# The first modulation rows of a two-block transformer kernel, loaded and summed in three column chunks instead of one

## The reference, cut to what matters

```
c_act = silu(c)                                  # 2048 numbers
mod   = c_act @ w_ada + b_ada                    # w_ada: 2048 x 12288, float32
sh1, sc1, gt1, sh2, sc2, gt2 = split(mod, 6)     # 2048 each
h = rms_norm(x, g_mix) * (1 + sc1) + sh1
z = h @ w_in                                     # w_in: 2048 x 11344
```

## Time and profile before

| | |
|---|---|
| three runs | 2665.74, 2667.66, 2667.6 us |
| the profiled execution | 2666.06 us, of it span 2664.2 us |
| TensorE matmul busy | 2625.6 us (99%) |
| VectorE busy | 1798.2 us (67%) |
| ScalarE busy | 1297.8 us (49%) |
| read from memory | 582.07 MB, 219 GB/s over the span |

### The profile page before, as it was taken

How to read it: one execution, slowest core, us unless ns; L and a number is a source line. 1 busy time by engine, 2 the same in 40 slices (tenths; PEclk the granted TensorE clock), 3 DMA queues, 4 the chain that set the end, 5 groups by cost and what they waited for, 6 DMA issues and landing times.

```text
span 2664.2 us, 33329 instructions
## 1 busy us (share of the span) xinstructions
PE 2625.6 (99%) x12045; PEld 2164.4 (81%) x12045; DVE 1798.2 (67%) x2072; ACT 1297.8 (49%) x1574; POOL 230.2 (9%) x164
## 2 busy tenths in 40 slices
PE   5999999999999999999999999999999999999999
PEld 3888887888888888888888887887888888888887
DVE  7978777878776677776766855677555555555554
ACT  4455544455454444444444554556454444444443
POOL 0000000100000000000001210240001111111110
PEclk9999999999999999999999999999999999999999
DMA  9989768678867766666665666644666666666663
GB/s 382 401 308 340 243 209 281 196 237 283 304 211 241 220 220 219 218 218 216 218 195 177 198 178 181 190 143 132 199 186 193 190 189 189 190 190 191 191 191 134
DMA packets 280792, 585.61 MB, mean 220 GB/s; under 512 B 22033, under 2 KB 24493, under 8 KB 279797
## 3 DMA queue, kind: packets, MB, share of 16 engines
q1 hardware_dynamic: 280340, 583.61, 68.1%
q10 hardware_dynamic: 352, 0.71, 0.1%
HBM read 582.07 MB, written 2.11 MB: 219 GB/s over the span
## 4 chain that ended last, share of the span: by engine, by line
PE 96%; DVE 2%; DMA 1%; ACT 0%; issue 0%; DVEq 0%; ACTq 0%
PE lin L499 30%; PE lin L501 30%; PE lin L500 30%; DMA sb_ada<-in_w_ada_dram 1%; PE aux L812 1%; PE aux L499 1%; PE aux L501 1%; PE aux L500 1%; PE aux L533 1%; PE aux L986 0%; PE aux L823 0%; DVE sb_wlo L1617 0%; DVE sb_acc L1708 0%; PE aux L557 0%; PE aux L999 0%
## 5 line engine op out<-in xcount | busy, mean ns | idle before, releaser
L1617 DVE TENSOR_TENSOR sb_wlo<-sb_raw,sb_whi 128x1024 fp32r<-128x1024 f32 x896 | 1114.8, 1247 | 784.8 <-ACT sb_whi L1041 781.2
L1041 ACT ACTIVATE sb_whi<-sb_raw 128x1024 fp32r<-128x1024 f32 x896 | 948.9, 1060 | 1237.2 <-PE lin L501 1159.1
L499 PE MATMUL lin<-sb_whi,sb_act_hi 128*128 128x512 f32 x2620 | 1038.4, 396 | 1.9 <-DVE sb_wlo L1617 1.0
L501 PE MATMUL lin<-sb_whi,sb_act_lo 128*128 128x512 f32 x2620 | 1021.8, 390 | 0.0
L500 PE MATMUL lin<-sb_wlo,sb_act_hi 128*128 128x512 f32 x2620 | 1020.7, 390 | 0.0
L499 PEld LDWEIGHTS lin<-sb_whi,sb_act_hi 128*128 128x128 f32 x2620 | 492.5, 188 | 108.5 <-issue 9.3
L501 PEld LDWEIGHTS lin<-sb_whi,sb_act_lo 128*128 128x128 f32 x2620 | 492.1, 188 | 104.3
L500 PEld LDWEIGHTS lin<-sb_wlo,sb_act_hi 128*128 128x128 f32 x2620 | 492.7, 188 | 99.9 <-issue 1.9
L499 PE MATMUL lin<-sb_whi,sb_hid_hi 128*128 128x512 f32 x704 | 275.3, 391 | 0.0
L501 PE MATMUL lin<-sb_whi,sb_hid_lo 128*128 128x512 f32 x704 | 274.1, 389 | 0.0
L500 PE MATMUL lin<-sb_wlo,sb_hid_hi 128*128 128x512 f32 x704 | 274.0, 389 | 0.0
(11 more groups left out here) (362 smaller groups left out, 1819.5 us busy)
## 6 DMA issues: line engine op xcount, KB each, us to landing
sb_raw<-in_w_in_dram SPq DMA_DIRECT2D x176, 512.0 KB, 6.7
sb_raw<-in_ffn_w_gu_dram SPq DMA_DIRECT2D x176, 512.0 KB, 3.7
sb_ada_in<-in_w_ada_dram SPq DMA_DIRECT2D x128, 512.0 KB, 5.1
sb_raw<-in_gla_w_in_dram SPq DMA_DIRECT2D x96, 512.0 KB, 3.8
sb_raw<-in_w_gate_dram SPq DMA_DIRECT2D x88, 512.0 KB, 3.8
sb_raw<-in_w_up_dram SPq DMA_DIRECT2D x88, 512.0 KB, 4.4
sb_raw<-in_w_down_dram SPq DMA_DIRECT2D x88, 512.0 KB, 4.4
sb_raw<-in_ffn_w_down_dram SPq DMA_DIRECT2D x88, 512.0 KB, 3.6
```

What stands on the lines that cost most here:

```text
L499: pe.matmul(o, h, whi[:, w], start=first and q == 0, stop=False)
L501: m = pe.matmul(o, l, whi[:, w], start=False, stop=last and q == 1)
L1041: act.activation(whi[:, idx % RING * HALF:(idx % RING + 1) * HALF], raw[:, idx // 2 % RING, idx % 2 * HALF:(idx % 2 + 1) * HALF], ACT.Copy ...
L1617: dve.tensor_tensor(wlo[:, c], raw[:, idx // 2 % RING, idx % 2 * HALF:(idx % 2 + 1) * HALF], whi[:, c].bitcast(fp32), ALU.subtract).then_i ...
```

## The change

**Row pieces.** The columns of the six early blocks are cut in three chunks of two blocks. A row piece is now `[128, 2 x 256]`, 256 KB, and there are 48: 16 for each chunk, chunk after chunk. The slots are still six, so piece n waits until piece n - 6 has been used.

**Who sums them.** 25 pieces (`TENSOR_ROWS`) are multiplied by TensorE: four matmuls of a 128 x 128 block by one column of c, added up in PSUM (`row_columns`, L626). The other 23 are added by VectorE as before, 512 columns wide (`row_add`, L1785, L1787). `chunk_columns` adds VectorE's accumulator to the same PSUM columns. Eight of TensorE's pieces stand ahead of the turns of x, three between them, and 14 in front of the matmuls of halves 0 to 6 (`ROWS_BEHIND`). VectorE's pieces of chunks 1 and 2 stand behind the splits of halves 0 to 6 (`ADDS_AT`).

**Order of halves.** The first three groups begin pair by pair: halves 0 to 2 are pair 0 of three groups, 3 to 5 pair 1, 6 to 8 pair 2; from half 9 on it is group after group as before. The modulation of pair 1 is made at half 3, that of pair 2 at half 6.

**SyncE's queue.** x is first, then 8 pieces, half 0, 8 pieces, half 1, and so on; late pieces begin after half 7 instead of half 4, the late sums are turned into columns behind half 39 instead of half 38. VectorE scales one of the two token blocks of x. The `keep_running` matmuls and the parameter loads ahead of phase A are gone or moved behind half 8 and half 12.

Between the splits of halves 5 and 6 now stand four adds (pieces 37, 38, 40 and 41), between that of half 6 and the modulation three (43, 44 and 46); ahead of the split of half 5 there are two (34 and 35). The core of the diff:

```
+CHUNKS = ((0, 2), (2, 4), (4, EARLY), (EARLY, KT))
+ROWS_BEHIND = {0: (17, 19), 1: (21, 23), 2: (25, 27), 3: (29, 31), 4: (33,), 5: (36,), 6: (39, 42, 45, 47)}
+ADDS_AT = {0: (16, 18), 1: (20, 22), 2: (24, 26, 28, 30), 3: (32,), 4: (34, 35), 5: (37, 38, 40, 41), 6: (43, 44, 46)}
+PIECES_FROM = (0, 8, 16, 24, 32, 37, 42, 48)
...
+        def row_piece(n):
+            if n >= SLOTS:
+                row_taken(n - SLOTS)
+            kt, c = n % KT, n // KT
+            sp.dma_start(ada0[:, n % SLOTS, :].rearrange("p (b n) -> p b n", b=2), w_first[kt * P:(kt + 1) * P, :, 2 * c * P:2 * (c + 1) * P]
+                         ).then_inc(sem(f"ada0_in{n % SLOTS}"), 16)
+        def row_taken(n):
+            if n in TENSOR_ROWS:
+                sp.wait_ge(sem("ada0_T"), row_on_tensor(n))
+            else:
+                sp.wait_ge(sem("ada0_sum"), VECTOR_ROWS.index(n) + 1)
...
+        sp.dma_start(X[:], tokens(A["x"][0])).then_inc(sem("x_in"), 16)
+        for n in range(PIECES_FROM[1]):
+            row_piece(n)
+        for i in range(A_ENDS[-1]):
+            first_half(i)
+            if i + 2 < len(PIECES_FROM):
+                for n in range(PIECES_FROM[i + 1], PIECES_FROM[i + 2]):
+                    row_piece(n)
...
+        def row_columns(n):
+            kt, c = n % KT, n // KT
+            pe.wait_ge(sem(f"ada0_in{n % SLOTS}"), 16 * (n // SLOTS) + 16)
+            if all(m >= n for m in TENSOR_ROWS if m // KT == c):
+                pe.matmul(column_banks[c][:, 0:4], ident, nothing, start=True, stop=False)
+            for j in range(4):
+                m = pe.matmul(column_banks[c][:, j:j + 1], ada0[:, n % SLOTS, j * P:(j + 1) * P], cact[:, kt:kt + 1], start=False, stop=False)
+            m.then_inc(sem("ada0_T"), 1)
...
+            for n in ROWS_BEHIND.get(i, ()):
+                row_columns(n)
+            if i in (A_HELD, 2 * A_HELD):
+                chunk_columns(i // A_HELD)
+            if p == made:
+                made += 1
+                pe.wait_ge(sem("tt_lo"), made)
+            half(0, "A", A_ENDS[-1], i, 0, 2 * p, first, last, banks=banks)
...
+        for g in range(A_PAIRS):
+            hk.setdefault(A_HELD * g, []).append(lambda g=g: early_pair(g))
+        for i, adds in ADDS_AT.items():
+            for n in adds:
+                hk.setdefault(i, []).insert(len(hk.get(i, ())) - (i == 6), lambda n=n: row_add(n))
```

More of the change, by code:

```diff
@@ L254, in build_program @@
     csg = small[:, 96:112]
+    nothing = small[:, 184:188]
     ss, ssy = small[:, 112:114], small[:, 114:116]
@@ L313, in ada_chunk @@
             if n < 2:
[L314 removed]
+                sp.wait_ge(sem("gs_made"), 4)
             if before >= 0:
@@ L363, in _ @@
                 sp.dma_start(relb[:], A["rel_bias"]).then_inc(sem("rel_in"), 16)
[L364 to L368, removed]
+            if LATE_FROM <= i < LATE_FROM + 2 * KT:
+                late_piece(i - LATE_FROM)
+            if i == 32:
                 sp.wait_ge(sem("erow_held"), 1)
@@ L565, in _, with chunk_columns, late_columns @@
         pe.wait_ge(sem("par_cols"), 1)
[L566 to L583, removed]
+        column_banks = (lin[0][1], aux[0], aux[1], aux[1])
+        def row_columns(n):
[6 more added lines that the diff above has]
+            m.then_inc(sem("ada0_T"), 1)
+        def chunk_columns(c):
+            pe.wait_ge(sem("ada0_sum"), sum(n < (c + 1) * KT for n in VECTOR_ROWS))
+            for j in range(4):
+                b, k = j // 2, 2 * c + j % 2
+                m = pe.matmul(column_banks[c][:, j:j + 1], acc0[:, b, k * P:(k + 1) * P], ones[:, 0:1], start=False, stop=j == 3)
+            m.then_inc(sem("ada0_T"), 1)
+        def late_columns():
+            pe.wait_ge(sem("ada0_sum"), EARLY_ROWS + 2 * KT)
+            pe.wait_ge(sem("par_cols"), 2)
+            pe.wait_ge(sem("erow_held"), 1)
+            for j in range(2 * LATE):
+                c = j % LATE * P
+                m = pe.matmul(aux[1][:, j * (WIDE // 4):(j + 1) * (WIDE // 4)], acc1[:, j // LATE, c:c + P], ones[:, 0:WIDE // 4], start=True, stop=True)
             m.then_inc(sem("ada0_T"), 1)
@@ L589, in keep_running, with late_parameters @@
                 pe.matmul(lin[0][0][:], ident, con[:, 0:NB], start=True, stop=True)
[L591 to L600, removed]
+        def late_parameters():
+            pe.wait_ge(sem("par_in"), 8 * 16)
+            for n, rws in ((1, 120), (2, 116)):
+                m = pe.transpose(aux[0][:, n % 2 * P:n % 2 * P + rws], parr[0:rws, n, :], ident[0:rws, 0:rws])
+            m.then_inc(sem("par_T"), 1)
+            pe.wait_ge(sem("rel_in"), 32)
+            pe.matmul(aux[1][0:NH, :], relb[:], onehot[:], start=True, stop=True).then_inc(sem("par_T"), 1)
+        pe.wait_ge(sem("csg_made"), 2)
+        for n in TENSOR_ROWS[:8]:
+            row_columns(n)
+        pe.wait_ge(sem("xs_made"), 2)
+        for g in range(KT // 2):
+            turn(X, g)
+            if g in (1, 3, 5):
+                row_columns(TENSOR_ROWS[8 + g // 2])
+        chunk_columns(0)
+        pe.wait_ge(sem("tt_free"), KT // 2)
         def project_ix():
@@ L654, in _ @@
         first_banks = (lin[1], lin[0], aux[2:4])
[L655 to L666, removed]
+        made = 0
+        for i, (g, p, a, first, last) in enumerate(A_HALVES):
+            n = a - A_DRAINS
+            banks = lin[n % 2] if n >= A_HELD else first_banks[a % 3]
+            if first and a >= 3:
+                pe.wait_ge(free0, A_DRAINS + 1 + n if n >= A_HELD else a)
+                pe.wait_ge(free1, A_DRAINS + 1 + n if n >= A_HELD else a)
+            for n in ROWS_BEHIND.get(i, ()):
+                row_columns(n)
+            if i in (A_HELD, 2 * A_HELD):
[4 more added lines that the diff above has]
+            half(0, "A", A_ENDS[-1], i, 0, 2 * p, first, last, banks=banks)
+            if i == 12:
+                late_parameters()
             if i == LATE_SUMMED:
-                pe.wait_ge(sem("ada0_sum"), EARLY_ROWS + 2 * KT)
-                first_columns(2)
-            if i == A_ENDS[0] - 1:
+                late_columns()
+            if i == A_ENDS[0]:
                 project_ix()
-            if i == A_ENDS[0] + 2:
+            if i == A_ENDS[0] + 3:
                 wix_turn()
```

169 lines of the change are left out of this document (85 added, 84 removed).

## The result

The changed kernel takes 2708.5 us (median of six runs, 2707.9 to 2710.1) against 2667.4 for the kernel before: ratio 1.0157, 95% interval 1.0146 to 1.0167. That is 41 us slower. The direction was forecast, the size was not: 2691 was expected and 2700 was the end of the range.

The account below looks back on a forecast made before the run. TensorE, 99% busy, was taken as the bound, so its waits cost in full. Half 6 16.9 to 22.9 us later, plus 1.7 clock and 1.5 VectorE, gave 20.1 to 26.1; 25 taken, 2691 us, range 2677 to 2700.

Parts of the forecast that it names:

- x: Start: x, now first in SyncE's queue, lands at about 10.6 us and is scaled at 18.8.
- The eight pieces: TensorE ahead of the turns of x: 0.90 or 1.8 us each, ending at 19.7 or 25.7, the second taken.
- The turns: Start, up to ScalarE's last copy: 6.4 us for turning x plus 2.7 for three pieces between, ending at 28.8 to 34.8.
- the late end: Half 0's start, forecast at 33.8 to 39.8 us: the later figure, with the eight pieces at the lower clock.
- TensorE's 14 pieces among these halves mostly lie in those waits: Halves 0 to 6: TensorE's pieces, 0.9 to 1.8 us each, mostly fall in waits for halves.
- Landing 4.4: Halves 2 to 6: each lands 4.4 us after issue, 3.7 with a nearly free queue plus 0.67 for one piece ahead.
- the steps: Half 0 to half 6: chain of issues, landings, splits and adds through six slots and one queue, 47.8 us.
- Behind half 6: After half 6 begins: 1.7 us lost to the lower clock, 1.5 to VectorE's pace (2.82 a half against TensorE's 2.73).
- the late end of the steps: Half 6's start, forecast 16.9 to 22.9 us later than before (81.6 to 87.6 against 64.72): the larger figure.
- Pieces slower than their rows: Rival, halves 0 to 8: one-column matmuls at the lower clock, each pair change throws it back; +33 to +40, 2703; chance 0.07.
- Slots free in time: Rival, pieces 16 to 47: SyncE never stops, half 6 at 68.8, or 56 to 62 if more hides, 2661; chance 0.08.
- The signs: Next profile: half 0 at 33 to 40, half 3 near 55, half 6 past 78, TensorE wait over 8, DMA not full.

Follow-up runs that it names:

- both: Changed kernel with twelve slots for row pieces instead of six and halves 0 to 6 issued ahead of piece 16: 2687.6 us, ratio 1.0078.
- warm: Changed kernel with four filler matmuls of 512 columns on TensorE after the constants land, ahead of the first eight pieces: 2710.0 us, ratio 1.0161.
- free_33_39: Changed kernel with row pieces 33 and 39 added by VectorE instead of multiplied by TensorE: 2702.2 us, ratio 1.0135.
- start_vec: Changed kernel with one row piece on TensorE ahead of half 0 instead of eleven, VectorE adding the other fifteen: 2699.0 us, ratio 1.0119.
- hold: Changed kernel with filler matmuls of 384 columns in TensorE's waits ahead of halves 3, 5 and 6: 2702.5 us, ratio 1.0133.
- spread: Changed kernel with ten row pieces on TensorE, twelve slots, pieces 0 to 15 ahead of half 0, then four between halves: 2673.9 us, ratio 1.0025.
- small_packets: Kernel before with each of sixteen early row pieces loaded as three transfers with 1 KB runs instead of one with 3 KB: 2671.7 us, ratio 1.0016.
- wide_hold: Changed kernel with two chunks, 16 + 16 pieces, seven on TensorE, twelve slots, filler ahead of halves 0 and 3, late pieces from half 4: 2669.8 us, ratio 1.0010.

## Why the prediction fell short

The mechanism was in the main the one forecast: SyncE's queue, the slots and the landings tie half 6 down, and taking that away (`both`) brings back 21 of 41 us. What was wrong is which engine lets a slot go last, and the clock at which TensorE works in this stretch. The sum was 25 and the loss 43 by the profiles. Step by step:

*x.* Scaled at 19.8, forecast 18.8. Right but for 1 us.

*The eight pieces.* They end at 26.8, forecast 19.7 or 25.7 with the second taken. Right in size, and only half for the reason given, an engine that comes from idling. In those rows the turns themselves came to the upper rate; here 64 records of one column did not, and in `warm`, where the engine did not come from idling, the clock fell under them.

*The turns: failed, 3.4 us.* I took 6.4 us from rows 9 and three pieces at 0.9. Both were prices of the upper clock, in a stretch that stands behind 13 us of one-column matmuls; measured are 12.5 us up to ScalarE's last copy, pieces included, against 9.1. If eight pieces were slow, what follows them could not be counted as fast. Half 0 came at 43.8, 4.0 behind the late end.

*"TensorE's 14 pieces among these halves mostly lie in those waits": failed, 7.4 us.* I looked at what the pieces cost TensorE and priced it at nothing. What they cost is the slot: piece 33 is multiplied behind half 3, which runs at the lower clock after its wait (5.0 us from 65.36 on), and piece 39, so half 5, stands behind it; piece 39 behind half 5 does the same to piece 45 and half 6. The prediction named VectorE's adds, of 34 and 35 and of 37 to 41, as the last releases; TensorE was later both times, and at half 3 too, where piece 25 lets piece 31 go (54.02 us in the chain). `free_33_39` shows it for 33 and 39.

*Landing 4.4: failed, about 4 us.* The lone half of rows 12 and one piece ahead was too little. While half 5 was on its way (72.97 to 78.57) the windows count 1.5 MB, nearly three times its bytes, at 230 to 340 GB/s: pieces issued on either side share the engines. With the late releases of 33 and 39 gone the loop takes 54.1 us (`free_33_39`), against 47.8 by the steps, 6.3 more. The landings of halves 4, 5 and 6 stand in its chain (6.2, 4.7, 6.3 instead of 4.4), 4.0 of these. Another 2.5 come ahead of half 4's issue, 16.1 us behind half 0 instead of 13.6, and there the chain goes through TensorE and not through a landing: half 0 at the lower clock (4.8 us) and the pieces in front of halves 1 to 3. The column sum takes 1.9 instead of 0.9; other steps were 1.2 shorter. All this is read from one run's times; the landings were not varied alone, so their share is argued and not shown.

*Behind half 6.* One stretch at the lower clock, 2.7 instead of 1.7; VectorE's pace, 0 instead of 1.5. Together near the forecast, by luck. By luck too the moved parameter loads are not seen: their matmuls behind half 12, priced at nothing, cost 1.3 us, and the kernel before lost about as much between halves 29 and 37.

So 22.9 (the late end of the steps) + 4.0 (half 0) + 7.4 + 6.3 is the 40.6 at half 6, plus 2.7.

*The rivals.* "Pieces slower than their rows" (2703, chance 0.07) came nearest in size and is half true: at the start the pieces run at the lower rate, among the halves two pieces take 1.84 us behind a half at the upper clock, and one behind a wait 1.70 or 1.87. It is rather the start that it describes; removing it gives 9.5 us (`start_vec`). Halves 3, 5 and 6 each stand behind a wait of 3 to 6 us and each begin at half the rate. The Trainium skill's rule that a wait between two groups of matmuls can throw the next one back to the lower clock (TensorE: Matmul & The Clock Gate, HAM oscillation — how this bites in real kernels) agrees with them; `hold` values it here at 6 us. "Slots free in time" had 35 us from half 0 to half 6; `both` took 39.0, so that working was nearly sound; in the changed kernel its condition was not met.

*The signs.* Half 0 by 40 us and half 3 near 55 failed (43.8 and 65.4); half 6 past 78, a long wait of TensorE ahead of it and DMA engines that are not full came true.

The range was too narrow for a plain reason: 47.8 us of the sum were a chain of five rounds through four engines, with one duration for each step, taken from a quiet stretch; the bounds let the landings only get shorter (3.2 us, where the shortest of a half in any chain looked at here took 4.4) and gave the pieces only their own time.

## What to carry to other kernels

Where a buffer slot is released by an in-order engine, price the whole queue ahead of the releasing instruction at the clock that it will have, not the instruction. Where a start waits for bytes at full DMA rate, cutting it finer pays in shorter runs and in gaps; count the bytes moved up to a fixed point before counting the waits. A step measured in a quiet, fully clocked stretch is more likely too short than too long in a chain that makes its engines wait.

## What the runs showed of the hardware

- TensorE's granted clock stood at the lower level from 16.1 to 50.3 us in `warm`, while the engine ran one-column matmuls, turns and half 0 without a gap from 15.07 on. In the changed kernel the same stretch shows 1.00 in the clock column and 0.21 us a record: before the first change on record the column does not tell the level, the records do.
- Full DMA engines moved 328 to 342 GB/s in `spread` and `small_packets`, where most runs are 1 KB, 384 to 395 in `wide_hold` with 2 KB, 389 with 3 KB in the kernel before, and 402 with the 2 KB of halves and the 5 KB of late pieces.
- The median packet took 49 ns with 1 KB (`small_packets`, 20 to 40 us), 126 with 3 KB (the kernel before, same window), 86 with 2 KB and 201 with 5 KB (the kernel before, 60 to 100 us).
